# A hybrid decoder trunk: the first norm computed on raw rows and by column groups, the second mixer's rows loaded in steps, two clearings moved

## Chip, core and metric

The kernel runs on one core of a Trainium2 chip as one program. Its time is the device time of that core in microseconds (us), the median of several executions; lower is better. All five compute engines and their DMA queues run their own instruction lists and meet through semaphores.

## What is computed

One layer of a decoder trunk over 1072 tokens of width 1024: 16 meta and 1024 prompt tokens as one sequence, and 8 decoding sequences of 4 tokens. An RMS norm, one wide input projection, four token mixers (HGRN2, RWKV-7, GLA, mLSTM), a gated sum of their projections, an output projection, and an MLP. In outline:

```
h    = x * rsqrt(mean(x*x) + 1e-6) * norm_mix
z    = h @ w_in                       # 1024 x 7704: mixer inputs and gates
o_b  = mixer_b(z), b = 0..3           # chunkwise recurrences with states in and out
x   += (sum_b sigmoid(z_gate_b) * (o_b @ w_branch_b)) @ w_out
hn   = rms(x, norm_mlp);  x += relu(hn @ w_up)**2 @ w_down
y    = rms(x, norm_final)
```

The change touches the first two lines, and in the mixers only the order of loads and of two clearings. `norm_mix` is a factor per channel and the root a factor per token, so both can be applied on either side of a product with `w_in`.

## The kernel before

Activations lie transposed: 8 rows (k = 0..7) of 128 channels by W = 1074 token columns, in three column groups of 358. A **chunk** is a product of all 8 rows with 128 output columns of the weights. TensorE does each product in float32 by three passes of a faster format (`three`, L477): both operands are split into a high part (a rounded copy) and a low part (the difference). A row of a chunk is 3 groups x 3 passes = 9 matmuls. Weights come through a ring of two slots (u = 0, 1); SyncE loads a slot once TensorE has finished its last chunk, ScalarE makes the high part (`weight_hi`, L467), GpSimd the low part in place (`weight_lo`, L472). Chunk u = 0 accumulates in PSUM banks 0 to 2 and u = 1 in 3 to 5; ScalarE copies them out (`evac`, which releases `banks_free`). Plain float32 products count as two passes each in the profile.

**The start.** SyncE loads constants, the 8 rows of x, the small weights WS (68 output columns: GLA's gate input and mLSTM's two gates), ring slot 0, the masks as float32 (into the second half of tile OT), the other constants and ring slot 1. ScalarE squares each row into four buffers used in turn (`rms_act`), VectorE adds them by two, TensorE sums over channels with a matrix of ones, 12 matmuls (`rms_pe`, L567), and ScalarE forms the root RST of all 1074 columns (L614, L616). Only then VectorE scales row after row by `norm_mix` and RST (L2061), ScalarE makes its high part (L1611), VectorE its low part (L627). TensorE does for each row first the small projection (L1035, three float32 matmuls) and then the row of chunk 0, then the whole of chunk 1. ScalarE copies the small projection into GA, passes the first barrier, makes the high part of chunk 2's weights (L467), four operations on mLSTM's gate rows (L1637 to L1641), and copies chunk 0 out (L1631 to L1633). Chunk 2 starts once chunk 0's banks are free and its weights split.

**The rows of the second mixer** (GLA and HGRN2 together). While mLSTM's tiles run, further chunks are filled in on TensorE column group by column group (`fill_work`; `fill_out` copies each group out of PSUM banks 6 and 7, and a whole row goes to the DRAM scratch `proj`). GpSimd's DMA queue brings the rows back: two first, then, when row 9 has been stored, the other eight at once behind the stores of mLSTM's states, and then tile after tile of v (`load_v`).

**Tiles and clearings.** The second mixer runs over 8 tiles of 128 tokens and a tail that also holds the decoding sequences. In each tile GpSimd prepares for TensorE a product by head for each of 7 levels (`gl_by_head`, L861, L863) and a weight's low part in between. After tile 4 it clears SGL (9 segments x 512 columns, the states of the tail) and issues 8 loads of states. In the RWKV mixer it clears RSTL (9 x 256) during the second tile, then loads states.

Of the kernel before, what the change touches and what calls it, by code (L numbers as in the profile page):

```python
# [55 lines left out]
def constants():  # L56
# [52 lines left out]
    xr xr_ready y_done y_out y_ready rows0 rows1 rows2 rows3 zeroed  # L109
# [32 lines left out]
def build(nc, A, OUT, fcols, ucols, fdim, udim):  # L142
    ctx = ExitStack()
    with ctx:
# [55 lines left out]
        def col(name, j=0, rows=P, lo=0):  # L200
            o, _ = COLS[name]
            return CC[lo:rows, o + j:o + j + 1]
# [62 lines left out]
        SQB = OT[:, 0:4]  # L265
        CUF = OT[:, 4:KD].rearrange("p k t -> p (k t)")[:, 0:udim]
# [15 lines left out]
        EMM = a.take(t=TILES + 1, h=4)  # L282
        MC = a.take(s=4, t=P)
# [4 lines left out]
        MATT = a.take(h=4, t=P)  # L288
        MKH = a.take(c=P)
# [145 lines left out]
        SUMS_OF_6 = KD - 1 + KD // 2 + 5  # L435
# [127 lines left out]
        def rms_pe(e):  # L563
            for i in range(KD // 2):
                e.wait_ge(S("norm_sum"), i + 1)
                for g in range(3):
                    last = e.matmul(PS(g, 0, GRP), ones, SQB[:, (2 * i) % 4, g * GRP:(g + 1) * GRP],  # L567
                                    start=i == 0, stop=i == KD // 2 - 1)
                last.then_inc(S("sq_used"), 1)

        def sum_pe(e, n, sq, bank):

            e.wait_ge(S("norm_sum"), n * (KD - 1) + KD // 2)
            for g in range(3):
                last = e.matmul(PS(bank + g, 0, G2), ones, sq[:, 0, part2(g)], start=True, stop=True)
            last.then_inc(S("sq_used"), 1)

        def group_sum_pe(e, g):

            e.wait_ge(S("norm_sum"), SUMS_OF_6 + (2, 4, 5)[g])  # L580
            if g == 2:
                e.wait_ge(S("rstd"), 3)
            last = e.matmul(PS(6 + g % 2, 0, G2), ones, SQ3[:, 0, part2(g)], start=True, stop=g < 2)
            if g == 2:
                e.wait_ge(S("norm_sq"), 2 * KD + 6 + 2 * (g + 1))
                last = e.matmul(PS(6, 0, G2), ones, SQ4[:, part2(g)], start=False, stop=True)
            last.then_inc(S("sq_used"), 1)

        def square(e, sq, n, k, src):

            if k >= 2:
                e.wait_ge(S("norm_sum"), (n - 1) * (KD - 1) + k - 1 + KD // 2)
            e.activation(sq[:, min(k, 1), T2], src[:, T2], ACT.Square, scale=D ** -0.5).then_inc(S("norm_sq"), 1)

        def add_square(e, sq, n, k):

            e.wait_ge(S("norm_sq"), n * KD + k + 1)
            if k > 1:
                e.wait_ge(S("norm_sum"), (n - 1) * (KD - 1) + k - 1 + KD // 2)
            e.tensor_tensor(sq[:, 0, T2], sq[:, 0, T2], sq[:, 1, T2], ALU.add).then_inc(S("norm_sum"), 1)  # L600

        def rms_act(e, st):
            for k in range(KD):
                e.wait_ge(S(f"x{k // 2}"), 32)
                if k >= 4:
                    e.wait_ge(S("sq_used"), (k - 4) // 2 + 1)
                e.activation(SQB[:, k % 4], XT[:, k, :], ACT.Square, scale=D ** -0.5).then_inc(S("norm_sq"), 1)
# [87 lines left out]
        def _(e):  # L695
# [5 lines left out]
            e.dma_start(WS, A["w_small"]).then_inc(S("ws"), 16)  # L701
# [55 lines left out]
        def pool_program(e):  # L757
# [12 lines left out]
            for u in range(2):  # L770
                weight_lo(e, u, P_ML)
# [78 lines left out]
            def gl_by_head(n, w, halves, between=None):  # L850
# [3 lines left out]
                for l in range(1, len(halves) + 1):  # L854
# [10 lines left out]
                    if l == 3 and between is not None:  # L865
                        between()
            def gl_tile(n):
                gl_by_head(n, P, HALVES, lambda: weight_lo(e, 1, n + (P_FILL + Q_GL_TILES)))
# [69 lines left out]
            e.wait_ge(S("rw_copied"), 3)  # L938
            e.memset(RSTL, 0.0).then_inc(S("zeroed"), 1)
# [71 lines left out]
            for g in range(3):  # L1011
                for v, sq in enumerate((SQ3[:, 1], SQ4)[:1 if g == 2 else 2]):
                    e.wait_ge(S("norm_sq"), 2 * KD + 6 + 2 * g + v + 1)
# [13 lines left out]
        def _(e):  # L1027
            e.wait_ge(S("consts"), 32)
            rms_pe(e)

            e.wait_ge(S("ws"), 64)
            for k in range(KD):
                e.wait_ge(S("ht_ready"), k + 1)
                for g in range(3):
                    last = e.matmul(PS(3 + g, 0, GRP)[0:68], WS[:, k, :], XT[:, k, g * GRP:(g + 1) * GRP],  # L1035
                                    start=k == 0, stop=k == KD - 1)
                if k == KD - 1:
                    last.then_inc(S("small"), 1)
                if k == 0:
                    e.wait_ge(S("split0"), P_ML + 1)  # L1040
                e.wait_ge(S("ot_ready"), k + 1)
                for g in range(3):
                    last = three(e, PS(g, 0, GRP), 0, k, slice(g * GRP, (g + 1) * GRP), k == 0, k == KD - 1)
            last.then_inc(S("chunk_done0"), 1)
            arrive(e)

            pe_chunk(e, 1, P_ML, P_ML)
# [508 lines left out]
            e.wait_ge(S("rstd"), 2)  # L1556
# [47 lines left out]
        def _(e):  # L1604
# [4 lines left out]
            for k in range(KD):  # L1609
                e.wait_ge(S("ht_ready"), k + 1)  # L1610
                e.activation(HT_R[:, k], XT[:, k, :], ACT.Copy).then_inc(S("hi_parts"), 1)  # L1611
            weight_hi(e, 1, P_ML)
            e.wait_ge(S("small"), 1)
            e.activation(row3(GA[0:16, :]), cols3(3)[0:16], ACT.Copy)
# [1367 lines left out]
```

## Time and profile before

| | |
|---|---|
| median of 3 executions (lowest, highest) | 2144.61 us (2144.0, 2159.99) |
| profiled execution, its own time | 2163.3 us |
| its span, first to last instruction | 2161.3 us |
| mean granted clock of TensorE | 0.978 of 2.4 GHz |
| TensorE busy | 2077.3 us (96%), 15235 matmul instructions |
| VectorE busy | 1032.9 us (48%) |
| ScalarE busy | 607.2 us (28%) |
| GpSimd busy | 453.9 us (21%) |
| DMA | 177.96 MB, mean 82 GB/s |

PE is TensorE's matmuls, PEld its weight loads, DVE VectorE, ACT ScalarE, POOL GpSimd, SP SyncE; a q behind a name is that engine's sequencer or DMA queue. L477 is line 477 of the kernel. An idle time is put down to what released the instruction after it. Tile names are the program's allocations: AR is the large arena that holds x, the root and the mixers' tiles, CF the constants, PS the PSUM.

### The profile page before, as it was taken

How to read it: one execution, taken by the hardware profiler on the slowest of the kernel's cores; microseconds unless marked ns; L12 is line 12 of the kernel's file. 1: busy time of each engine (PE TensorE's matmuls, PEld its weight loads, DVE VectorE, ACT ScalarE, POOL GpSimd, SP SyncE). 2: the span in 40 equal slices, each digit the busy share in tenths (PEclk: the TensorE clock that was granted, in tenths of full speed). 3: DMA queues.
4: the chain of work that ended last, by engine and by line, in shares of the span. 5: the costliest groups of instructions: out<-in, count | busy, mean ns of one | idle time of the engine just before them, and what ended most of it. 6: DMA issues, size and time to landing. Idle time of an engine off the chain costs nothing.

```text
span 2161.3 us, 37070 instructions
## 1 busy us (share of the span) xinstructions
PE 2077.3 (96%) x15235; PEld 1967.6 (91%) x15235; DVE 1032.9 (48%) x1616; ACT 607.2 (28%) x821; POOL 453.9 (21%) x463
## 2 busy tenths in 40 slices
PE   6999999999999989998899899999999999999997
PEld 4999988999999878887789899999999999999996
DVE  4052333465655545454443685522222235565656
ACT  4432224332322254222222431101011023333343
POOL 1122113444653511100002572200000010000020
PEclk9999999999999989999998999999999999999999
DMA  4123225222221332111024662311111242111112
GB/s 169 40 61 85 60 90 163 81 69 65 65 66 64 132 113 80 32 42 42 22 61 150 218 194 87 111 57 49 39 49 59 89 168 101 49 44 44 49 39 100
DMA packets 50852, 177.96 MB, mean 82 GB/s; under 512 B 6481, under 2 KB 10033, under 8 KB 50497
## 3 DMA queue, kind: packets, MB, share of 16 engines
q1 hardware_dynamic: 25296, 85.77, 13.7%
q0 software_dynamic: 17648, 61.31, 8.3%
q10 hardware_dynamic: 7808, 29.41, 3.7%
q8 instruction: 81, 1.33, 0.3%
q14 instruction: 19, 0.15, 0.0%
HBM read 128.95 MB, written 47.51 MB: 82 GB/s over the span
## 4 chain that ended last, share of the span: by engine, by line
PE 85%; DVE 7%; issue 3%; DMA 3%; ACT 2%; POOL 0%; DVEq 0%; SPq 0%; ACTq 0%; POOLq 0%
PE PS L477 29%; PE PS L649 22%; PE PS L1565 16%; PE PS L1537 2%; PE PS L1172 2%; DMA RING<-in_w_all 1%; DVE AR L2602 1%; DMA RING<-in_w_br 1%; PE PS L1184 1%; PE PS L1035 1%; PE PS L1207 1%; PE PS L1200 1%; DVE CF_parts L623 1%; PE PS L1253 1%; PE PS L1292 0%
## 5 line engine op out<-in xcount | busy, mean ns | idle before, releaser
L477 PE MATMUL PS<-HT_parts,WHIA_parts 128*128 128x352 f32 (+1 forms) x1440 | 517.1, 359 | 12.3 <-POOL RING_parts L472 6.6
L477 PE MATMUL PS<-OT_parts,WHIA_parts 128*128 128x352 f32 (+1 forms) x1440 | 477.5, 332 | 0.0
L477 PE MATMUL PS<-HT_parts,RING_parts 128*128 128x352 f32 (+1 forms) x1440 | 476.5, 331 | 0.0
L472 POOL TENSOR_TENSOR RING_parts<-RING,WHIA_parts 128x1024 fp32r<-128x1024 f32 x60 | 160.6, 2676 | 711.8 <-ACT WHIA_parts L467 711.8
L477 PEld LDWEIGHTS PS<-HT_parts,WHIA_parts 128*128 128x128 f32 x1440 | 279.4, 194 | 29.0 <-issue 12.7
L477 PEld LDWEIGHTS PS<-OT_parts,WHIA_parts 128*128 128x128 f32 x1440 | 279.8, 194 | 4.0 <-issue 0.5
L477 PEld LDWEIGHTS PS<-HT_parts,RING_parts 128*128 128x128 f32 x1440 | 279.2, 194 | 0.0
L1565 PE MATMUL PS<-MIXHI_parts,CF_parts 128*128 128x352 f32 x786 | 253.8, 327 | 5.0 <-DVEq L2852 3.0
L649 PE MATMUL PS<-HT_parts,CF_parts 128*128 128x352 f32 x768 | 249.4, 325 | 0.9 <-ACT AR L616 0.9
L649 PE MATMUL PS<-HT_parts,RING_parts 128*128 128x352 f32 x768 | 249.5, 325 | 0.0
L649 PE MATMUL PS<-OT_parts,CF_parts 128*128 128x352 f32 x768 | 249.2, 325 | 0.0
L1565 PE MATMUL PS<-MIXHI_parts,RING_parts 128*128 128x352 f32 x768 | 248.7, 324 | 0.0
L1565 PEld LDWEIGHTS PS<-MIXHI_parts,CF_parts 128*128 128x128 f32 x786 | 147.6, 189 | 8.4 <-DVEq L2852 2.6
L2007 ACT ACTIVATE MIXHI_parts<-AR 128x1056 fp32r<-128x1056 f32 x94 | 102.2, 1088 | 166.3 <-PE PS L1565 160.6
L649 PEld LDWEIGHTS PS<-HT_parts,CF_parts 128*128 128x128 f32 x768 | 144.9, 189 | 1.3 <-ACT AR L616 1.2
L649 PEld LDWEIGHTS PS<-OT_parts,CF_parts 128*128 128x128 f32 x768 | 145.0, 189 | 0.1
L649 PEld LDWEIGHTS PS<-HT_parts,RING_parts 128*128 128x128 f32 x768 | 144.8, 189 | 0.0
L1565 PEld LDWEIGHTS PS<-MIXHI_parts,RING_parts 128*128 128x128 f32 x768 | 144.3, 188 | 0.0
L2811 DVE SCALAR_TENSOR_TENSOR AR<-PS,AR 128x1056 f32 (+1 forms) x32 | 40.3, 1258 | 191.0 <-PE PS L649 184.5
L1565 PE MATMUL PS<-CF_parts 128*128 128x352 f32 x378 | 122.8, 325 | 0.0
L1565 PE MATMUL PS<-LO_parts,CF_parts 128*128 128x352 f32 x372 | 120.1, 323 | 0.0
L623 DVE CAST CF_parts<-RING 128x1024 fp32r<-128x1024 f32 x80 | 63.2, 789 | 103.7 <-DMA RING<-in_w_all 80.4
(453 smaller groups left out, 3321.5 us busy)
## 6 DMA issues: line engine op xcount, KB each, us to landing
RING<-in_w_all SPq DMA_DIRECT2D x132, 512.0 KB, 3.7
AR<-gates POOLq DMA_DIRECT2D x32, 528.0 KB, 4.0
proj<-AR ACTq DMA_DIRECT2D x18, 537.0 KB, 5.3
AR<-proj POOLq DMA_DIRECT2D x18, 537.0 KB, 7.7
gates<-CF ACTq DMA_DIRECT2D x16, 528.0 KB, 5.3
gates<-AR ACTq DMA_DIRECT2D x16, 528.0 KB, 5.7
AR<-in_xT SPq DMA_DIRECT2D x8, 537.0 KB, 8.4
AR<-in_xT POOLq DMA_DIRECT2D x8, 528.0 KB, 5.5
```

Of the source, the lines that this page charges most:

```text
L472: e.tensor_tensor(RING_R[:, u], RING[:, u], WHIA_R[:, u].bitcast(F32), ALU.subtract).then_inc(S(f"split{u}"), 1)
L477: last = e.matmul(out, a_[:, u, k, :], b_[:, k, t], start=first and i == 0, stop=end and i == 2)
L623: return e.tensor_copy(hi, x)
L649: last = e.matmul(PS(3 * u + g, 0, G2), a_[:, u, k, :], b_[:, k, t], start=k == 0 and i == 0, stop=k == KD - 1 and i == 2)
L1035: last = e.matmul(PS(3 + g, 0, GRP)[0:68], WS[:, k, :], XT[:, k, g * GRP:(g + 1) * GRP], start=k == 0, stop=k == KD - 1)
L1172: last = e.matmul(PS(3 * (l % 2), lo * m, hi * m)[0:w], x[:, g, l, 0:w], GQB[:, l % 2, lo * m:hi * m], start=True, stop=True)
L1184: last = e.matmul(PS(3 * (l % 2) + b, c * w, c * w + w)[0:w], x[r, g, nl + 1, 0:w], q[r, g, 1, 0:w], start=True, stop=True)
L1200: e.matmul(PS(3, h * 64, h * 64 + 64)[0:w], att[:, ao:ao + w], v[:, h * 64:h * 64 + 64], start=h == 0, stop=False, skip_group_check=True)
L1537: last = e.matmul(PS(3 * u + tg, 0, G2), a_[:, v, k, :], b_[:, k, t], start=k == 2 * br and i == 0, stop=k == 2 * br + 1 and i == 2)
L1565: last = e.matmul(PS(3 * v + g, 0, G2), a_[:, u, 4 * v + r % 4, :], b_[:, part2(g)], start=r == 0 and i == 0, stop=r == 31 and i == 2)
L2007: e.activation(AHI_R[r % 2][:, T2], act_row(r)[:, T2], ACT.Copy).then_inc(S("act_hi"), 1)
L2811: e.scalar_tensor_tensor(row2(dst), cols2(3 * u), 0.0, row2(RST2), ALU.max, ALU.mult).then_inc(S(f"banks_free{u}"), 1)
```

## The change

Six edits. (1) WS is scaled by `norm_mix` and the small projection runs on the raw rows, four of them before the sums over channels and four behind; its result is multiplied by the root afterwards. (2) The squares have a buffer each; VectorE adds them up in two trees, the last row in three column groups, so that TensorE needs 6 matmuls with ones instead of 12; the root is formed group by group. (3) TensorE does rows 0 to 4 of chunk 0, then rows of chunk 1 and chunk 0 by turns; the low parts of the first two ring slots move from GpSimd to VectorE; both slots and WS are loaded earlier, the masks go in two pieces to another place. (4) Six of the eight rows of the second mixer are loaded by two and two before and between other work, two are left behind the wait. (5) SGL is cleared in thirds inside tile 5 and its states are loaded behind that tile; tiles 6 and 7 are written out instead of looped. (6) The clearing of RSTL waits for the second RWKV tile's solved values (`rw_us`). Renumbered semaphore counts and the new places of the masks are left out here. In the diff `small(k)` is the small projection of row k and `row(u, k)` the nine matmuls of row k of a chunk; `clear_segments` is called behind levels 4, 5 and 6 of tile 5; VectorE scales row 0 in three groups, each behind its part of the root.

```diff
@@ helpers
+        SQB = [OT[:, k] if k < 4 else HT[:, k] for k in range(KD)]
+        SQ_SUM = SQB[0], SQB[4]
...
+        def rms_pe(e, part):
+            if part == 0:
+                e.wait_ge(S("norm_sum"), 3)
+                for g in range(3):
+                    e.matmul(PS(g, 0, GRP), ones, SQ_SUM[0][:, g * GRP:(g + 1) * GRP], start=True, stop=False)
+                return
+            for g in range(3):
+                e.wait_ge(S("norm_sum"), 4 + 2 * (g + 1))
+                e.matmul(PS(g, 0, GRP), ones, SQ_SUM[1][:, g * GRP:(g + 1) * GRP],
+                         start=False, stop=True).then_inc(S("sq_used"), 1)
...
         def rms_act(e, st):
-            for k in range(KD):
+            for k in range(KD - 1):
                 e.wait_ge(S(f"x{k // 2}"), 32)
-                if k >= 4:
-                    e.wait_ge(S("sq_used"), (k - 4) // 2 + 1)
...
+            for g in range(3):
+                t = slice(g * GRP, (g + 1) * GRP)
+                e.activation(SQB[KD - 1][:, t], XT[:, KD - 1, t], ACT.Square, scale=D ** -0.5).then_inc(S("norm_sq"), 1)
             weight_hi(e, 0, P_ML)
-            e.wait_ge(S("sq_used"), KD // 2)
-            rstd(e, st, row3(RST), cols3(0)).then_inc(S("rstd"), 1)
+            for g in range(3):
+                e.wait_ge(S("sq_used"), g + 1)
+                rstd(e, st, RST[:, g * GRP:(g + 1) * GRP], PS(g, 0, GRP)).then_inc(S("rstd"), 1)
+
+        def rms_sums(e):
+            def add(a_, b_, t=slice(0, W)):
+                e.tensor_tensor(SQB[a_][:, t], SQB[a_][:, t], SQB[b_][:, t], ALU.add).then_inc(S("norm_sum"), 1)
+            for i in range(2):
+                e.wait_ge(S("norm_sq"), 2 * i + 2)
+                add(2 * i, 2 * i + 1)
+            e.wait_ge(S("norm_sum"), 2)
+            add(0, 2)
+            e.wait_ge(S("norm_sq"), 6)
+            add(4, 5)
+            for g in range(3):
+                t = slice(g * GRP, (g + 1) * GRP)
+                e.wait_ge(S("norm_sq"), KD + g)
+                add(6, 7, t)
+                e.wait_ge(S("norm_sum"), 4 + 2 * g + 1)
+                add(4, 6, t)
@@ SyncE
             for k in range(KD):
                 e.dma_start(XT[:, k, :], xs[k]).then_inc(S(f"x{k // 2}"), 16)
-            e.dma_start(WS, A["w_small"]).then_inc(S("ws"), 16)
+                if k == 0:
+                    e.dma_start(WS, A["w_small"]).then_inc(S("ws_in"), 16)
...
             load(0, A["w_all"], 0)
-            e.dma_start(CUF, A["cu"]).then_inc(S("ws"), 16)
+            load(1, A["w_all"], 1)
             e.dma_start(CF[:, first:], A["cf"][:, first:]).then_inc(S("ws"), 16)
-            load(1, A["w_all"], 1)
+            e.dma_start(CUF0, A["cu"][:, 0:CU_CUT]).then_inc(S("ws"), 16)
+            e.dma_start(CUF1, A["cu"][:, CU_CUT:]).then_inc(S("ws"), 16)
@@ GpSimd
-            for u in range(2):
-                weight_lo(e, u, P_ML)
             arrive(e)
...
             e.wait_ge(S("states_final"), 1)
+            for u in range(2):
+                e.wait_ge(S(f"fill_sent{u}"), (Q_RW - 1) * 16)
+            for i, dst in ((6, GQ[:, 2]), (7, GK[:, 2])):
+                e.dma_start(dst, proj_row(i)).then_inc(S("rows1"), 16)
+            for i, slot in ((4, 0), (5, 1)):
+                e.dma_start(OTG[:, slot], proj_row(i)).then_inc(S("rows2"), 16)
             for h in range(4):
...
+            for i, dst in ((0, GQ[:, 0]), (1, GQ[:, 1])):
+                e.dma_start(dst, proj_row(i)).then_inc(S("rows1"), 16)
             weight_lo(e, 1, P_FILL + Q_RW)
             for u in range(2):
                 e.wait_ge(S(f"fill_sent{u}"), Q_RW * 16)
-            for i, slot in ((4, 0), (5, 1), (8, 2), (9, 3)):
+            for i, slot in ((8, 2), (9, 3)):
                 e.dma_start(OTG[:, slot], proj_row(i)).then_inc(S("rows2"), 16)
-            for i, dst in ((0, GQ[:, 0]), (1, GQ[:, 1]), (6, GQ[:, 2]), (7, GK[:, 2])):
-                e.dma_start(dst, proj_row(i)).then_inc(S("rows1"), 16)
...
             with e.Fori(0, 5) as n:
                 gl_tile(n)
-            e.memset(SGL, 0.0).then_inc(S("zeroed"), 1)
+            def clear_segments(i):
+                if i < 3:
+                    ins = e.memset(SGL[:, 3 * i:3 * i + 3], 0.0)
...
+            gl_tile(5, clear_segments)
             e.wait_ge(S("zeroed"), 5)
             load_states()
-            with e.Fori(5, TILES - 1) as n:
+            for n in range(6, TILES):
                 gl_tile(n)
-            gl_tile(TILES - 1)
...
             e.wait_ge(S("rw_copied"), 3)
+            e.wait_ge(S("rw_us"), 2)
             e.memset(RSTL, 0.0).then_inc(S("zeroed"), 1)
@@ TensorE
+            e.wait_ge(S("ht_ready"), 1)
+            for k in range(4):
+                small(k)
+            rms_pe(e, 0)
+            rms_pe(e, 1)
+            for k in range(4, KD):
+                small(k)
             arrive(e)
-            pe_chunk(e, 1, P_ML, P_ML)
+            for k in range(5):
+                row(0, k)
+            for k in range(5, KD):
+                row(1, k - 5)
+                row(0, k)
+            e.wait_ge(S("ws"), 64)
+            for k in range(3, KD):
+                row(1, k)
@@ ScalarE
             for k in range(KD):
-                e.wait_ge(S("ht_ready"), k + 1)
+                e.wait_ge(S("ht_ready"), k + 2)
                 e.activation(HT_R[:, k], XT[:, k, :], ACT.Copy).then_inc(S("hi_parts"), 1)
+                if k == 2:
+                    weight_hi(e, 1, P_ML)
+                if k == 3:
+                    e.wait_ge(S("small"), KD)
+                    e.activation(row3(GA[0:68, :]), cols3(3)[0:68], ACT.Copy).then_inc(S("banks_free1"), 1)
@@ VectorE
+            e.wait_ge(S("ws_in"), 16)
+            e.tensor_tensor(WS, WS, bc(col("norm_mix", 0, P, 0, KD).unsqueeze(2), WS.shape), ALU.mult).then_inc(S("ht_ready"), 1)
+            rms_sums(e)
+            weight_lo(e, 0, P_ML)
...
             for k in range(KD):
+                e.wait_ge(S("small"), k + 1)
...
                 if k == 4:
+                    weight_lo(e, 1, P_ML)
             h_lo(KD - 1)
+            e.wait_ge(S("banks_free1"), 1)
+            e.tensor_tensor(GA[0:68, :], GA[0:68, :], RST[0:68, :], ALU.mult)
```

## Rows read from the trace of the kernel before

**Rows 1.** Waits of TensorE (line, tile, releaser: us in total, times, longest us)
```profile
PE PS L477 <- POOL RING_parts L472: 6.6, 2, 4.4
...
PE PS L1385 <- DVE AR L2607: 5.0, 8, 2.5
...
PE PS L477 <- ACTq L1618: 2.0, 1, 2.0
```

**Rows 2.** Chain that ended last, 0 to 60 us (start us, us, what)
```profile
2.39 6.19 DMA AR<-in_xT
...
12.22 3.45 PE PS L567 x6
...
27.11 3.82 PE PS L1035 x6
...
33.00 1.81 PE PS L1035 x6
...
34.81 1.48 PE PS L477 x9
...
57.95 2.12 PE PS L477 x10
```

**Rows 3.** Timeline, 44 to 100 us (start us, us, engine, line, operation [idle before])
```profile
56.17 51.18 SPq L704 DMA_DIRECT2D RING<-in_w_all  x5
...
66.26 0.21 ACT L1633 ACTIVATE AR<-PS 128x32 f32<-128x32 f32 x1
...
71.58 0.77 ACT L1631 ACTIVATE AR<-PS 128x716 f32<-128x716 f32 x1 [5.12 <-PE PS L477]
```

**Rows 4.** Timeline, 0 to 44 us
```profile
11.40 2.09 ACT L607 ACTIVATE OT<-AR 128x1074 f32<-128x1074 f32 x2 [0.71 <-DMA AR<-in_xT]
...
29.32 1.33 DVE L2061 SCALAR_TENSOR_TENSOR AR<-AR,CC 128x1074 f32<-128x1074 f32 x1
...
31.76 1.33 DVE L2061 SCALAR_TENSOR_TENSOR AR<-AR,CC 128x1074 f32<-128x1074 f32 x1
```

**Rows 5.** Windows of 1 us (busy us and instructions by engine, granted clock, DMA)
```profile
60.00:61.00 1.00, 1.00 (x5) 1.00 (x4) 0.00 (x0) 0.97 (x2) 0.21 (x1) 0.50 0.00 0
```

**Rows 6.** Chain that ended last, 340 to 400 us
```profile
360.59 12.50 DMA RING<-in_w_all
...
376.65 23.45 PE PS L477 x132
```

**Rows 7.** DMA issues, 318 to 425 us (count, KB each, median us to landing)
```profile
AR<-proj POOLq DMA_DIRECT2D x8, 537.0 KB, 13.4
...
RING<-in_w_all SPq DMA_DIRECT2D x6, 512.0 KB, 4.4
```

**Rows 8.** Timeline, SyncE's queue, 318 to 425 us
```profile
346.58 73.52 SPq L704 DMA_DIRECT2D RING<-in_w_all  x6
```

**Rows 9.** Timeline, VectorE and GpSimd, tiles of the second mixer
```profile
386.08 0.43 DVE L2304 COPY AR<-AR 128x384 f32<-128x384 f32 x1
...
566.14 0.77 POOL L861 TENSOR_TENSOR AR<-AR,CF 128x128 f32<-128x128 f32 x2 [0.99 <-PE PS L1172]
...
583.00 3.98 POOL L879 MEMSET AR<- 128x4608 f32 x1
...
585.50 1.76 DVE L2304 COPY AR<-AR 128x384 f32 x1
```

**Rows 10.** Timeline, VectorE, GpSimd and ScalarE, second and third RWKV tiles
```profile
902.84 4.76 DVE L2602 COPY AR<-AR 32x128 f32<-32x128 f32 x4
...
904.96 2.11 POOL L939 MEMSET AR<- 128x2304 f32 x1
...
916.68 0.39 ACT L1920 ACTIVATE AR<-PS 128x256 f32<-128x256 f32 x1 [6.85 <-PE PS L1400]
...
936.90 3.03 DVE L2602 COPY AR<-AR 32x128 f32<-32x128 f32 x4
```

**Rows 11.** Chain that ended last, whole span
```profile
965.92 2.26 DVE AR L2602
```

More of the change, by code:

```diff
@@ L198, in mask8, with col @@
             return CU[0:rows, o + k * w:o + (k + 1) * w]
-        def col(name, j=0, rows=P, lo=0):
+        def col(name, j=0, rows=P, lo=0, n=1):
             o, _ = COLS[name]
-            return CC[lo:rows, o + j:o + j + 1]
+            return CC[lo:rows, o + j:o + j + n]
         ZS = CF[:, fcols["bd_ml"][0]:fcols["bd_ml"][0] + W]
@@ L282, in build @@
         EMM = a.take(t=TILES + 1, h=4)
+        CU_CUT = 4 * P + 4 * P + P + 4 * P + 4 * P
+        CUF0 = Arena(a.at).take(c=CU_CUT)
         MC = a.take(s=4, t=P)
@@ L288, in build @@
         MATT = a.take(h=4, t=P)
+        CUF1 = Arena(a.at).take(c=udim - CU_CUT)
         MKH = a.take(c=P)
@@ L561, in evac @@
             emit(3 * u).then_inc(S(f"banks_free{u}"), 1)
-        def rms_pe(e):
-            for i in range(KD // 2):
-                e.wait_ge(S("norm_sum"), i + 1)
+        def rms_pe(e, part):
+            if part == 0:
+                e.wait_ge(S("norm_sum"), 3)
                 for g in range(3):
-                    last = e.matmul(PS(g, 0, GRP), ones, SQB[:, (2 * i) % 4, g * GRP:(g + 1) * GRP],
-                                    start=i == 0, stop=i == KD // 2 - 1)
-                last.then_inc(S("sq_used"), 1)
+                    e.matmul(PS(g, 0, GRP), ones, SQ_SUM[0][:, g * GRP:(g + 1) * GRP], start=True, stop=False)
[4 more added lines that the diff above has]
+                         start=False, stop=True).then_inc(S("sq_used"), 1)
         def sum_pe(e, n, sq, bank):
-            e.wait_ge(S("norm_sum"), n * (KD - 1) + KD // 2)
+            e.wait_ge(S("norm_sum"), n * (KD - 1) + SUMS0)
             for g in range(3):
@@ L864, in gl_by_head, with gl_tile, between @@
                                     ALU.mult).then_inc(S("gl_qb"), 1)
[L865 to L868, printed above, removed]
+                    if between is not None:
+                        between(l)
+            def gl_tile(n, clear=None):
+                def between(l):
+                    if l == 3:
+                        weight_lo(e, 1, n + (P_FILL + Q_GL_TILES))
+                    elif l > 3 and clear is not None:
+                        clear(l - 4)
+                gl_by_head(n, P, HALVES, between)
                 weight_lo(e, 0, n + (P_FILL + Q_GL_TILES + 1))
@@ L1028, in _, with small @@
             e.wait_ge(S("consts"), 32)
-            rms_pe(e)
-            e.wait_ge(S("ws"), 64)
-            for k in range(KD):
-                e.wait_ge(S("ht_ready"), k + 1)
+            def small(k):
+                e.wait_ge(S(f"x{k // 2}"), 32)
                 for g in range(3):
@@ L1036, in _, with row @@
                                     start=k == 0, stop=k == KD - 1)
-                if k == KD - 1:
[L1038 to L1044, printed above, removed]
-            arrive(e)
-            pe_chunk(e, 1, P_ML, P_ML)
+                last.then_inc(S("small"), 1)
+            def row(u, k):
+                if u == 0:
+                    e.wait_ge(S("ot_ready"), k + 1)
+                if k == 0:
+                    e.wait_ge(S(f"split{u}"), P_ML + 1)
+                    if u == 1:
+                        e.wait_ge(S("banks_free1"), P_ML + 1)
+                for g in range(3):
+                    last = three(e, PS(3 * u + g, 0, GRP), u, k, slice(g * GRP, (g + 1) * GRP), k == 0, k == KD - 1)
+                if k == KD - 1:
+                    last.then_inc(S(f"chunk_done{u}"), 1)
+            e.wait_ge(S("ht_ready"), 1)
[5 more added lines that the diff above has]
+                small(k)
+            arrive(e)
+            for k in range(5):
[6 more added lines that the diff above has]
+                row(1, k)
             for p in range(P_ML + 1, P_FILL):
@@ L2805, in _ @@
                     split_chunk(e, u, i + P_OUT + 1)
[L2807 removed]
+            e.wait_ge(S("rstd"), 4)
             def relu(i, u, dst):
```

64 lines of the change are left out of this document (29 added, 35 removed).

## The prediction

> **What bounds the kernel now.** I read part 1 of the page first: TensorE is busy 96% of the span, so an edit is worth only what it takes out of TensorE's own waiting, the slow matmuls behind such a wait, or matmuls. Then the list of TensorE's waits [rows 1], to see which waits the diff touches, and last the chain and the timeline at each such place. There are four: the start, where few matmuls run until the norm is known [rows 2]; the hand-over from chunk 0 to the next ones; a ring load that arrives late beside the mixer's rows; and the two clearings on GpSimd. The chain that ends last leads through TensorE at all four, and behind each of them TensorE's order is full again, so time saved there comes off the end.
>
> **The sum's base.** The profiled execution took 2163.3 us, its span 2161.3; the median of the three runs is 2144.6, 18.7 less. The gains below come from the profiled one, and I take them off the median unscaled.
>
> **Part 1, the start.** Before, the chain is: rows land, squares, adds, 12 ones-matmuls, root, scaling, and only then small projection and chunk 0 by turns, 1.81 + 1.48 us a row [rows 2]. Chunk 1 ends when its copy can start, at 71.6 [rows 3]. I work out the same point for after.
> Rows land: the first pair at 8.6 (2.39 + 6.19) [rows 2], the second at 11.4 [rows 4], so 2.8 us a pair. The small weights (272 KB, half a row) now stand behind row 0 and push all by 0.8: 9.4, 12.2, 15.0, 17.8. Two squares take 2.09 [rows 4], so seven and three thirds end at 20.1; the DVE adds of the last row come in thirds (two of about 0.5 each, an estimate by size from the 1.33 of a whole row's scaling [rows 4]), so the three sums are ready at 20.4, 21.5 and 22.5. TensorE meanwhile does small(0 to 3) from 9.4: at the slow pace 3.45 us hold six passes, at the fast one 1.81 [rows 2], so 3.6 + 3 x 1.8 = 9.0, till 18.4; six ones-matmuls follow, the last ending at 23.2, then small(4 to 7), 4 x 1.81, till **30.45**. The DVE does not wait for that: after the last third of the root (about 24.3) it scales row 0, and ScalarE's copy and the low part make it ready at 27.8; each next one costs 2.44 (31.76 - 29.32) [rows 4]: rows 1 to 3 at 30.3, 32.7, 35.2. The low part of ring 1, now on DVE (about 1.2, by size from the same 1.33), puts row 4 at 38.8. TensorE does rows 0 to 3 till 36.6, waits 2.2, and then has two chunks to draw on: five and three rows of chunk 0, with three of chunk 1 between, till 49.25; the five left of chunk 1 till 56.65. The drop of the clock behind a wait of 2 us is seen before: after 2.0 of it [rows 1], from 57.95, the eight rows of chunk 1 should take 8 x 1.48 = 11.8 and took 13.6 [rows 2, 3], with 0.50 granted at 60 (1.2 GHz of 2.4) [rows 5]. I charge 1.5 for the wait of 2.2: chunk 0 ends at 50.75.
> What is late next: chunk 2 needs chunk 0's banks. Before, the load issued at 56.2, ScalarE's high part, four 4-row operations and three copies followed one another until 66.5, 10.5 after chunk 0's end (57.95 - 2.0) [rows 1 to 3]; that was hidden under chunk 1, whose 12 us are now cut to 7.4. So chunk 2 starts at 50.75 + 10.5 = 61.25 after a wait of about 3, plus another 1.5 of slow matmuls: 62.75 against 71.6. **Gain 8.8.** Bounds: 11.8 with no drop at all, 1 if the slow pace holds through small(0 to 3) and the ones (about 8 more). I take the middle reckoning because the clock did rise within the first six passes before.
> The other edits here: WS's scaling on DVE (about 0.7) lies before the sums; scaling GA by the root (1.27) and the mask copy in two parts move to DVE's end, at about 48, before ScalarE needs the barrier; POOL is released from two low parts. Cost 0 under that cover, at most 2.5 without. SP issues both ring loads ahead of the constants, which are wanted from 47 on only.
>
> **Part 2, the second mixer's rows.** The ring load issued at 360.6 took 12.5 us [rows 6], against a median of 4.4 for the six of this stretch, while eight rows of 537 KB took a median of 13.4 [rows 7]. TensorE waited 4.4 for the low part behind it [rows 1] and then ran slow for about 12 matmuls; as above that is 1.6. After, four rows are issued at about 346 and two behind the state stores, and only rows 8 and 9, the tile of v, the load and one store (about 2.4 MB) are under way at 360.6, against 5.7 MB before. In proportion the load takes 12.5 x 2.4/5.7 = 5.3, lands at 366, say 367 with what is left of the state stores, and its chunk is ready 3.6 later (376.65 - 373.09) [rows 6], at 370.6; TensorE wants it 4.4 before 376.65, at 372.2. **Gain 6.0**, bounds 0 and 6.0.
> Queued behind it: on POOL the six row issues (about 0.55 each) stand before the low part of ring 1. That chunk's load starts at 346.6 [rows 8] and now shares with four rows and a store, 3.3 MB: at 5.7 MB in 12.5 us it lands near 354 instead of 351, and the chunk is ready at 357.6. It is wanted three column groups (8 x 1.48/3 = 3.95 each) ahead of 372.2, at 360.4, so it fits, by almost 3 us. ScalarE waits those 3 us and has no work that TensorE wants before. DVE's wait for the rows becomes shorter.
> The Trainium skill (DMA: Bandwidth & Descriptors, Queues, rings and completion order) says that a DMA engine goes round robin between the queues. By that rule the ring load has a third of the engines whatever the number of rows, and the sum would lose this term. The 12.5 us speak against it here.
>
> **Part 3, clearing SGL.** The whole clearing took 3.98 on GpSimd, and DVE's copy of 128x384 took 1.76 beside it, 0.43 elsewhere [rows 9]; the norm that TensorE transposes next stands behind that copy on DVE, so the 1.3 are TensorE's. In thirds of 1.33 it falls beside DVE's predicated copies from PSUM. At level 7 GpSimd idles 0.99 waiting for TensorE [rows 9], so the three pieces eat the slack and push a little. Bounds of the push 0 and 4.0; I take 0.3, since idle time stands before levels 6 and 7. **Gain 1.0.** The eight state loads (5 us of issuing) move behind tile 5, where the weight's low part and the same issue stood before; the states are wanted in the tail only.
>
> **Part 4, clearing RSTL.** It ran 904.96 to 907.07, and DVE's four small copies took 4.76 beside it, against 3.03 in the next tile [rows 10]. TensorE's wait was 2.5 where the eight tiles together have 5.0 [rows 1], and the tile lasted 34.06 (936.90 - 902.84) against 29.02 for the next (965.92 - 936.90) [rows 10, 11]: 2.0 of waiting and 3.0 of slow clock. Held until the second tile's RUS, it runs from 917.1 (916.68 + 0.39) to 919.2 [rows 10]. **Gain 5.0**, bounds 2 and 5.0. GpSimd's next work is the low part of a later weight, over 10 us off.
> The Trainium skill (SBUF — State Buffer, Who interferes with whom) says that a GpSimd instruction and a DVE copy or tensor_scalar with both ports exclude each other for its whole length. The trace agrees (4.76 against 3.03). By it a small DVE operation at 919.0 would wait 0.2.
>
> **Sum.** 8.8 + 6.0 + 1.0 + 5.0 = 20.8; the profiled execution would be 2142.5, the median **2123.8**.
>
> **Rivals.**
> - *The start gives little*: the slow pace lasts, or the chain to chunk 0's banks waits longer. For it: slow matmuls from 12.2 and again from 27.1 [rows 2]. Against: a rise each time. It gives 1 to 4 instead of 8.8: 2130. Chance 0.14.
> - *The ring load stays slow*: what delays it is any traffic on GpSimd's queue, and 1.3 MB is still issued there at 359. Against: it is a quarter of before. 2123.8 + 6.0 = 2129.8. Chance 0.12, the skill's rule in it.
> - *More than reckoned*: the hand-over drops no clock and row 4 is not waited for. 2123.8 - 3.0 = 2120.8. Chance 0.15.
> - *The clearings find a new victim*: thirds push levels 5 to 7, or the held one blocks DVE's tail work. 3 to 5 lost: 2128. Chance 0.07.
> - *The clock stays down through the start* (slower). DVE feeds a row each 2.44 us and TensorE needs 1.48, 61% busy. Should that keep 1.2 GHz until chunk 1 ends, every pass costs double from 9.4 on: smalls 2 x 14.5, ones 7.2, 16 rows at 2.7: about 88.6, which is 17 later than 71.6 rather than 8.8 earlier: 2123.8 + 25.8 = 2149.6. It decides once more than about 20 us of the gain go. Against: 2.4 GHz came back after 3.8 us at 27.1. Chance 0.03.
> - *Nothing is changed in effect*: 2144.6. Chance 0.02.
> The forecast keeps 0.47, own range 2118 to 2129.
>
> **Numbers.** The range reaches from the better case to the single losses and holds four cases in five: 2116 to 2132. One per cent of 2144.6 is 21.4, about what a measurement of this kernel can tell, so faster by over 1% means below 2123.2: the better case and a bit under half of the forecast, since it lies 0.6 from the line: 0.41. Slower by over 1%: 0.03. Within: 0.56.
>
> **What would show it.** Small projection on TensorE from about 9.4; chunk 2's first matmul at 61 to 63, behind a wait of about 3 us for ScalarE; no wait of over 1 us for a low part near 370 and a ring load of 5 to 7 us; DVE's copy at the sixth tile of GLA back at 0.43; the second RWKV tile at 29 us. Wrong if TensorE waits instead for the root, for a ring load near 355, or for the products by head.

## The result, and the profile after

| | kernel before | changed kernel |
|---|---|---|
| median of the comparison | 2152.1 us (10 runs, 2140.8 to 2160.0) | 2136.4 us (10 runs, 2128.7 to 2143.4) |
| profiled execution / its span | 2163.3 / 2161.3 | 2138.1 / 2136.5 |
| granted clock over the span | 0.978 | 0.983 |

The ratio is 0.9945, 95% interval 0.9925 to 0.9964: 11.8 us less (8 to 16), where 20.8 were forecast; the two medians lie 15.7 apart, inside that interval. Timed again later, the same kernel gave 0.995 (0.9926 to 0.9974). One execution of the kernel u2 below (2154.9 us) was in a slower state and is left out of its ratio. The two profiled executions lie 25 us apart, more than the medians, because the one of before was 11 us above its own median; so where single traces are compared below, several kernels with the same part stand side by side.

**The start.** From the chain of waits of the changed kernel, 0 to 62 us (start us, us, what):

```profile
9.80 10.35 PE PS L1079 x24
20.15 1.81 PE PS L572 x6
...
39.65 10.66 PE PS L481 x63
50.33 0.06 SPq L733
...
50.50 3.46 DMA RING<-in_w_all
...
60.54 0.09 ACT AR L1694
60.63 0.14 issue
60.77 1.23 PE PS L481 x3
```

The small projection (L1079) runs from 9.8; before, there was only waiting and twelve ones-matmuls until 27.1 [rows 2]. Chunk 0 ends at 50.3 (50.75 forecast), chunk 2's first matmul is at **60.77** (61.25 forecast; the step stood at 71.6 before [rows 3]).

**Waits of TensorE** (line, tile, releaser: us in total, times, longest us), which answer to [rows 1]:

```profile
PE PS L481 <- POOL RING_parts L476: 5.8, 2, 5.3
...
PE PS L481 <- ACT AR L1694: 3.1, 1, 3.1
PE PS L1448 <- DVE AR L2678: 3.0, 8, 0.6
```

The clearing of RSTL no longer costs TensorE a wait (2.5 longest before, 0.6 now). The wait for chunk 0's banks (3.1) was reckoned with. The first row speaks against the forecast: the wait for a low part near 370 was to vanish, and it grew from 4.4 to 5.3.

**The second mixer's rows.** The chain, 340 to 380 us, answers to [rows 6]:

```profile
351.21 13.35 DMA RING<-in_w_all
...
365.73 2.35 POOL RING_parts L476
368.08 0.04 issue
368.12 11.95 PE PS L481 x55
```

The ring load took 13.35 us, not the 5.3 of the forecast, though two rows and not eight are issued near it. By windows of 4 us (busy us and instructions of PE, PEld, DVE, ACT, POOL; granted clock, DMA share, GB/s):

```profile
344.00:348.00 4.00, 4.00 (x26) 4.00 (x26) 0.00 (x0) 2.06 (x4) 3.98 (x5) 1.00 1.20 393
348.00:352.00 4.00, 4.00 (x26) 4.00 (x25) 1.11 (x1) 3.34 (x5) 2.30 (x4) 1.00 1.28 57
352.00:356.00 4.00, 4.00 (x27) 4.00 (x26) 3.28 (x3) 3.56 (x3) 0.00 (x0) 1.00 0.75 38
356.00:360.00 4.00, 4.00 (x26) 4.00 (x25) 0.00 (x0) 0.00 (x0) 0.00 (x0) 1.00 0.90 331
```

From 348 to about 357 the DMA engines are reported busy and move 38 to 57 GB/s, a tenth of the 393 to 410 before and after. This **slow stretch** is the row to read: the ring load was not waiting for bytes ahead of it, everything was slow. What moved in 2 us of it, and in 2 us behind it (queue: packets, MB, share of 16 engines):

```profile
q0 software_dynamic: 16, 0.06, 80.0%
...
q0 software_dynamic: 154, 0.59, 72.9%
q1 hardware_dynamic: 31, 0.13, 16.3%
q10 hardware_dynamic: 25, 0.11, 13.0%
```

The first row is 352 to 354: GpSimd's queue alone (q0), each packet more than 1 us long, while the ring load (q1) and a filler store (q10) had been issued near 351 and moved nothing. The other three rows are 358 to 360. In the records of single packets the packets of the first row are the row loads' own, some 4 KB each; each of the four stores of state n (elements of 4 bytes) appears as 16 packets of 72 bytes, and these went out between 347.2 and 355.5.

**The clearing of RSTL** (start us, us, engine, line, operation), second RWKV tile, answers to [rows 10]:

```profile
893.65 2.96 DVE L2673 COPY AR<-AR 32x128 f32<-32x128 f32 x4
...
902.86 2.02 POOL L985 MEMSET AR<- 128x2304 f32 x1 [7.02 <-ACT AR L1981]
...
923.19 2.33 DVE L2673 COPY AR<-AR 32x128 f32<-32x128 f32 x1
```

DVE's copies take 2.96 instead of 4.76; the tile lasts 923.19 - 893.65 = 29.5 us instead of 34.1. At the sixth tile of GLA DVE's copy of 128x384 takes 0.41 (at 578.1; 0.43 forecast), and the three pieces of SGL are cleared behind it, from 593.0 to 599.7.

### The profile page after: what moved, and what is told of

Same layout as the page of the kernel before. It is cut to its first block, busy times and chain, and to the rows that moved or that the text cites. A ratio compares the mean times of both kernels' runs of the same rounds, so it can differ in the third digit from the quotient of the medians.

```text
span 2136.5 us, 37031 instructions
## 1 busy us (share of the span) xinstructions
PE 2067.6 (97%) x15223; PEld 1959.4 (92%) x15223; DVE 1038.5 (49%) x1629; ACT 605.1 (28%) x825; POOL 443.1 (21%) x463
## 4 chain that ended last, share of the span: by engine, by line
PE 85%; DVE 8%; DMA 3%; issue 2%; ACT 2%; DVEq 0%; POOL 0%; SPq 0%; ACTq 0%
PE PS L481 29%; PE PS L677 22%; PE PS L1628 16%; PE PS L1600 2%; PE PS L1235 2%; DMA RING<-in_w_all 1%; DVE AR L2673 1%; PE PS L1247 1%; DMA RING<-in_w_br 1%; PE PS L1270 1%; DVE OT_parts L655 1%; PE PS L1263 1%; DVE CF_parts L651 1%; PE PS L1316 1%; PE PS L1406 1%
## 5 line engine op out<-in xcount | busy, mean ns | idle before, releaser
L481 PEld LDWEIGHTS PS<-HT_parts,WHIA_parts 128*128 128x128 f32 x1440 | 278.2, 193 | 31.3 <-issue 12.6
L476 POOL TENSOR_TENSOR RING_parts<-RING,WHIA_parts 128x1024 fp32r<-128x1024 f32 x58 | 150.7, 2599 | 695.7 <-ACT WHIA_parts L471 695.7
L608 POOL TENSOR_TENSOR AR<-AR 128x1056 f32<-128x1056 f32 x12 | 29.4, 2449 | 392.5 <-ACT AR L601 392.5
```

The lines of the kernel that those rows point to most:

```text
L476: e.tensor_tensor(RING_R[:, u], RING[:, u], WHIA_R[:, u].bitcast(F32), ALU.subtract).then_inc(S(f"split{u}"), 1)
L481: last = e.matmul(out, a_[:, u, k, :], b_[:, k, t], start=first and i == 0, stop=end and i == 2)
```

## The experiments

The question: why did the ring load stay slow, and what is each part worth? Theory **H1**: the mLSTM's state stores (c, 32 x 9 pieces of 256 bytes for each head, and n, 32 x 9 elements of 4 bytes for each head; GpSimd's queue, just before) make the slow stretch. Rival **H2**: the row loads on that queue do.

**Chunk 0's banks first.** In ScalarE's order:

```diff
-            weight_hi(e, 0, P_ML + 1)
             e.wait_ge(S("zeroed"), 2)
 ...
+            evac(e, 0, 0, pre_conv(0))
+            weight_hi(e, 0, P_ML + 1)
             e.activation(RI, GA[32:36, :], ACT.Copy)
 ...
-            evac(e, 0, 0, pre_conv(0))
```

> The changed kernel, with ScalarE's copies of chunk 0's banks put ahead of the high part of the next weight and of the gate rows' four small operations. Theory: chunk 2's start is bound by ScalarE's order alone (load landed 53.98, high part, four small operations, three copies till 60.6), and TensorE's wait of 3.1 us there costs itself and some 3 us of slow clock in the chunks behind it. Then the copies end near 52.5, the low part of the weight near 57.5, the wait before chunk 2 falls to under 0.5 us, and the first transposes of the mLSTM, at 115.0 in the changed kernel, come at 109 to 112; the time is 3 to 6 us under the changed kernel's. Rival: the wait is for the weight's load and its low part on GpSimd (57.4), which come no earlier: the wait stays over 2 us, the transposes come at 115.

Measured: ratio to the kernel before 0.9897 (0.9836 to 0.9959). TensorE runs through; its chain from 45 us on:

```profile
44.88 64.08 PE PS L481 x389
108.96 1.97 PE PS L1123 x18
```

The transposes come at 109.0 against 115.0. The six us are the 3.1 of waiting and 3 of slow clock behind it. Over the ten traces that keep ScalarE's old order behind the changed start the transposes stand at 111.5 to 114.8, over the three with the new one at 108.8 to 109.2, so 2.5 to 6 is the fair figure. The theory holds at this place; the time agrees and says no more (0.0048 below the changed kernel's ratio, some 10 us, but from four runs, with an interval that holds the changed kernel's 0.9945).

**Is it the stores?** Four kernels, one profiled run each. The first leaves state c and n out but for eight pieces:

```diff
-  e.dma_start(OUT["mc"][:, h].rearrange("s k v -> k s v"), SML[r, :, h * 65:h * 65 + 64])...
-  e.dma_start(OUT["mn"][:, h].rearrange("s k -> k s"), SML[r, :, h * 65 + 64])...
+  e.dma_start(OUT["mc"][0:1, h, 0], SML[32 * h:32 * h + 1, 0, h * 65:h * 65 + 64])...
+  e.dma_start(OUT["mn"][0:1, h], SML[32 * h:32 * h + 1, 0, h * 65:h * 65 + 32])...
```

> The changed kernel without the mLSTM's state stores: each of the eight (four of c, whose pieces are 256 bytes, four of n, whose elements go out singly, 4 bytes each) is replaced by one piece of one partition, so that the counts stay; the states c and n of the output are left out. H1, the scattered stores slow the DMA engines for some 6 us and the ring load behind them waits for that: the ring load issued near 351 lands within 4 to 7 us instead of 13.35, TensorE's wait of 5.3 us for the low part goes to under 0.5, and its order from there on comes 5 to 7 us earlier. H2, the row loads issued on GpSimd's queue just before the ring load hold it back: it stays at 12 to 14 us. H1 also says that the loads of rows 4 to 7, issued ahead of the stores, land as before, and rows 0, 1, 8, 9 earlier by 5 us or more.

A miss: ring load 11.2 us, TensorE's wait 3.1. A slow stretch was there with eight tiny stores (1.5 KB in all), from about 346 to 350, shorter and less deep (73 to 159 GB/s by windows of 1 us).

The second stores state n in longer pieces:

```diff
-  e.dma_start(OUT["mn"][:, h].rearrange("s k -> k s"), SML[r, :, h * 65 + 64])...
+  e.dma_start(OUT["mn"][:, h], SML[32 * h:32 * h + 1, :, h * 65:h * 65 + 32])...
```

> The changed kernel with only the four stores of state n changed: 9 pieces of 128 bytes from one partition each, instead of 288 elements of 4 bytes (the values stored there are not n). If the 4-byte elements are what slows the engines, the ring load near 351 lands within 4 to 8 us, as without any of the stores. If the 1152 pieces of 256 bytes of state c are, it stays above 10. If H2 holds (the row loads before it), it stays at 12 to 14.

Ring load 6.2 us, TensorE's wait behind it 0.3. The windows of this kernel, for the ones above:

```profile
344.00:348.00 4.00, 4.00 (x26) 4.00 (x25) 0.00 (x0) 2.49 (x3) 4.00 (x6) 1.00 1.04 398
348.00:352.00 4.00, 4.00 (x26) 4.00 (x25) 2.69 (x3) 3.36 (x5) 0.67 (x1) 1.00 1.02 412
352.00:356.00 4.00, 4.00 (x27) 4.00 (x26) 3.76 (x8) 2.11 (x3) 0.00 (x0) 1.00 0.82 308
```

The same bytes, the same rows ahead of the load, the same 1152 pieces of 256 bytes of state c, and no slow stretch. Only the 4-byte pieces are gone (4 stores of 32 x 9 elements, 4.6 KB together). So it is these. The third holds three of the loads on GpSimd's queue back:

```diff
-            for i, slot in ((8, 2), (9, 3)):   # and load_v(0), ahead of the ring load
+            e.wait_ge(S("chunk_loaded0"), (P_FILL + Q_RW + 2) * 16)
+            for i, slot in ((8, 2), (9, 3)):
```

> The changed kernel with rows 8 and 9 and the first tile of v issued on GpSimd only once the ring load has landed; the state stores stay ahead of it. H1 (the scattered stores slow the engines): the ring load issued near 351 finds the same slow stretch and lands in 9 to 12 us, shorter only by the share that rows 8, 9 and v take after it; TensorE's wait stays over 2 us. H2 (row loads on GpSimd's queue issued shortly before it): it lands in 4 to 6 us and the wait is gone.

12.3 us, a little over H1's 9 to 12; TensorE waits 5.9. Six rows still stand ahead of the load here, so this run alone clears rows 8, 9 and v; it is the run before (e3), with every row load in its place and no slow stretch, that makes H2 fall. The fourth stores neither c nor n:

```diff
-  both state stores; the four waits on their count lowered by 8 x 16
```

> The changed kernel with none of the eight mLSTM state stores (c and n of the states are left out of the output), and the counts waited for lowered to match. The run that put one piece of one partition in place of each store kept a slow stretch (11.2 us for the ring load), the run that stored n in pieces of 128 bytes had none. If the slow stretch is made by stores whose data goes out 4 bytes at a time, and a single piece of one partition is cut up just so, then here the row loads move at over 400 GB/s from 345 on, the ring load issued near 350 lands in 4 to 7 us and TensorE's wait for the low part stays under 0.6. If the slow stretch has another cause (the rows read shortly after they were written, or the row loads themselves), it stays, and the load takes over 10 us.

7.3 us, a little over the 4 to 7 expected, with 417 to 421 GB/s from 345 to 350; TensorE's wait behind it is 0.3, as expected, though GpSimd took 3.4 us for that low part instead of 2.35. From 340 to 352, packets of the kernel with one piece for each store, then of this one:

```profile
DMA packets 1085, 3.18 MB, mean 265 GB/s; under 512 B 347, under 2 KB 347, under 8 KB 1084
...
DMA packets 1155, 4.39 MB, mean 366 GB/s; under 512 B 129, under 2 KB 129, under 8 KB 1154
```

That explains the miss. The records of single packets show what the eight pieces became: against the kernel without stores there are 64 more packets of 16 bytes, 64 more of 8 and 128 more of 4 (16 for each store, as for the other transfers of this queue). So a piece of a single partition was cut in 16, 256 bytes into 16 and 128 bytes into 8, and packets of 8 and 16 bytes made a slow stretch too, where the n stores of e3 went out as packets of 128 bytes and made none. What lies between 16 and 128 bytes was not tried, and why so few bytes slow everything stays open.

**What is each part worth?** Five kernels, each timed several times beside the kernel before.

```diff
 u1: parts 2, 3 and 4 undone (the start alone)
 u2: part 2 undone (all eight rows behind the stores and the low part)
 u34: parts 3 and 4 undone
   e.wait_ge(S("fill_sent..."), (Q_RW - 1) * 16)
-  rows 6, 7, 4, 5
   the eight state stores
+  rows 6, 7, 4, 5          (x7: stores first)
```

> Part 1 of the change alone: the rows of the second mixer, and both clearings, are as in the kernel before. If the start gives what the trace of the changed kernel shows (chunk 2 at 60.8 instead of 71.6, less some 3 us of slow clock behind the wait there), the time is 7 to 9 us below the kernel before (ratio 0.996), with the ring load near 351 at 12 to 14 us. Rival: the start's gain is eaten on the way, by waits for transfers that don't come earlier; then under 4 us are left (ratio over 0.998).

> The changed kernel with part 2 undone: all eight rows of the second mixer are issued behind the state stores and the low part again. If part 2 brought nothing, since the slow stretch behind the stores is what the ring load waits for, the time is that of the changed kernel within 2 us (ratio to the kernel before 0.993 to 0.996), with the ring load at 12 to 14 us. If the number of row loads matters beside it, as the prediction had it, the ring load takes over 15 us here and the time is 3 to 6 us above the changed kernel's (ratio 0.996 to 0.998).

> The changed kernel with parts 3 and 4 undone: SGL is cleared in one piece behind tile 4's loop, RSTL as soon as its place is free. By the traces the two are worth 1.9 and 4.6 us: the time is 5 to 8 us above the changed kernel's (ratio 0.997 to 0.999 to the kernel before), TensorE's waits for DVE are back (2.5 to 2.9 us longest, at the second tile of RWKV, and 1.3 to 2.9 at the sixth of GLA). Rival: the waits move elsewhere when removed, and the two are worth under 3 us.

> The changed kernel with rows 6, 7, 4 and 5 issued behind the eight state stores instead of ahead of them. Theory M: part 2 did not shorten the ring load because its four rows (2.1 MB) stand ahead of the stores on GpSimd's queue and push the 4-byte elements of n from 340 to 348 to 357, into the time of the ring load issued near 350. With the stores first the slow stretch is over by about 347, the ring load takes 6 to 10 us, TensorE's wait for the low part is under 2 us, and the time is 5 to 9 us below the changed kernel's (ratio to before 0.989 to 0.992). Rival: six rows issued before the ring load cost it as much as the slow stretch does (M is wrong, the bytes count); then it stays at 12 us or more and the time at the changed kernel's.

> The changed kernel itself, on the chip of the next three, so that they can be compared with it directly. Ratio to the kernel before 0.993 to 0.997, as measured before.

| kernel | median us | ratio to the kernel before, 95% |
|---|---|---|
| changed kernel again (same chip as x7, u34) | 2137.0 | 0.9950 (0.9926 to 0.9974) |
| u1: start alone | 2142.8 | 0.9976 (0.9954 to 0.9997) |
| u2: change without part 2 | 2123.4 | **0.9902** (0.9866 to 0.9937) |
| u34: change without the clearings | 2146.1 | 1.0000 (0.9975 to 1.0026) |
| x7: change with the stores first | 2127.1 | **0.9906** (0.9869 to 0.9943) |

The clearings were worth a little more than expected (9.1 by the medians, 5 to 8 expected), with TensorE's waits for DVE back at 2.9 in both loops; the start alone was worth a little less (5.5 for 7 to 9), and its ring load took 8.2, not 12 to 14. The third row is a surprise that both theories of that run missed: without part 2 the kernel is some 9 us *faster* ((0.9945 - 0.9902) x 2150; the two intervals overlap a little). x7 gives as much on the same chip (2137.0 - 2127.1 = 9.9; these two intervals overlap a little as well), by turning the order of twelve DMA issues. The ring load took 9.1 in u2 and 10.0 in x7, where u2's two theories had 12 to 14 and over 15. In x7 (its windows):

```profile
344.00:348.00 4.00, 4.00 (x27) 4.00 (x26) 0.67 (x1) 3.71 (x5) 4.00 (x6) 1.00 0.80 41
348.00:352.00 4.00, 4.00 (x26) 4.00 (x25) 3.73 (x3) 3.62 (x3) 0.23 (x1) 1.00 0.83 231
352.00:356.00 4.00, 4.00 (x27) 4.00 (x25) 0.00 (x0) 0.02 (x1) 0.00 (x0) 1.00 1.02 420
```

The stores go out at 334 to 339, the slow stretch lies at 340 to 349, the ring load issued at 347.6 takes 10.0, and TensorE's longest wait for the low part is 1.9. In the changed kernel four rows (2.1 MB) stand ahead of the stores on their queue and hold the 4-byte pieces back until about 347: part 2 carried the slow stretch into the ring load. The last n store lands at about 358 in the changed kernel (issued at 342.9, 15.4 us) and at about 349 in u2 (338.6, 10.8 us), and in both full speed comes back within 1 us of that. (x7's own late guest is ScalarE's silu, which waits 4.6 for rows issued into the slow stretch.)

One stretch shows it over fourteen traces: from the first matmul of the gate projection behind the mLSTM (L1206) to the first product of GLA tile 0 (L1235), both by their first start:

```
before                                              56.0
change; again; u34; banks first; rows 8, 9, v held  58.0  58.6  58.7  58.5  58.5
part 2 undone: u1; u2                               54.3  51.1
stores first: x7                                    54.3
eight tiny stores                                   53.2
no 4-byte pieces there (e3, e5 and two candidates)  50.4  50.3  50.4  51.2
```

Part 2 costs 4 to 7 us beside the changed start; with part 2 in, the 4-byte pieces cost 8. The rows cost something by themselves as well: in the second candidate below, with eight rows at once and no slow stretch (321 to 425 GB/s), the ring load takes 9.1 us and TensorE waits 1.1, in e3 6.2 and 0.3.

The clearings by tile. GLA, from the fourth tile to the sixth, around the clearing of SGL, by DVE's L2434: 77.3, 77.2 and 78.8 us where it runs in one piece (before, u1, u34), 74.6 or 74.7 in ten of the eleven others. Of the 77.3, only one belongs to the clearing: the tile that it disturbs lasts 38.5 there against 37.4 in the ten, and the other 1.6 lie in the tile ahead, whose clock is low (0.83 granted over 570 to 580) before the clearing begins at 583.0. In u1 and u34, where TensorE waits 2.9 and not 1.3, the disturbed tile lasts 40.0 and 41.6. RWKV, from the first tile to the third, by L2678: 63.1, 68.6 and 66.4 against 58.3 to 62.8 (mean 59.6). So part 3 is worth 1 to 4 us and part 4 from 3.5 to 9, both least in the trace of before; the timed difference of u34 (9 to 12 us) lies within their sum.

**Candidates.**

```diff
 chunk 0's banks first, and
-  e.dma_start(OUT["mn"][:, h].rearrange("s k -> k s"), SML[r, :, h * 65 + 64])   (POOL, x4)
+  ins = e.tensor_copy(MNK[r, :], SML[r, :, h * 65 + 64])                         (DVE, x4)
+  e.dma_start(OUT["mn"][:, h].rearrange("s k -> k s"), MNK[32 * h:32 * h + 32, :])
+      (POOL, one behind each of three later low parts, one before GLA tile 5)
```

> A candidate: the changed kernel with chunk 0's banks copied ahead of the next high part, and with state n copied by DVE into a small tile of its own (128x9), from which GpSimd stores it one quarter at a time, behind the low parts of three later weights and before tile 5 of GLA. Theory: the four n stores together slow all transfers for some 9 us; one at a time costs 2 to 3 us of transfers each, which no ring load with 8 us to spare feels. Then the ring load near 345 lands in 5 to 7 us, TensorE's wait for the low part (5.3 us) and the slow clock behind it go, and the time is 9 to 13 us below the changed kernel's (ratio to the kernel before 0.988 to 0.991). Rival: the waits only move, to the ring loads beside the later n stores (loads of 8 us or more and new waits for low parts at 365 to 400); then the gain over the changed kernel is only the 4 to 6 us of the copies' order.

> A candidate: the start and both clearings of the change, chunk 0's banks copied first, state n stored a quarter at a time from a tile of its own, and part 2 undone (all eight rows behind the ring load). If rows at full speed cost the ring load nothing worth naming, part 2 is neutral once the n stores are out of the way, and this is within 3 us of the candidate that kept part 2 (ratio 0.985 to 0.989). If the early rows help DVE and ScalarE to finish sooner, it is slower than that one by over 3 us (over 0.989); if they take the ring load's engines, it is faster (under 0.985).

Measured: with part 2 kept 2118.4 us, **0.987** (0.9839 to 0.9902); with part 2 undone 2116.1 us, 0.9884 (0.9839 to 0.9929). Both keep every output and beat both kernels: 16 to 21 us below the changed one, the first with an interval that does not touch its own (0.9925 to 0.9964). The ring load of the story took 8.4 and 9.1 us, longer than the 5 to 7 expected of the first, but no slow stretch lay beside it (235 GB/s or more until the last 2 us), and TensorE's waits there are 0.3 and 1.1. The loads beside the later quarters of n took 6.6 to 7.8 us. With the n stores apart part 2 is neutral, within what these runs tell.

## Why the prediction was wrong

**Part 1, the start: right.** Every station came within 1.3 us up to chunk 2 (small projection 9.8 for 9.4; ones till 22.0 for 23.2; chunk 0's end 50.3 for 50.75; chunk 2 at 60.8 for 61.25). The slow clock fell in behind the wait of 3.1 rather than behind the 1.8 for row 4, and cost 3 where 1.5 + 1.5 were charged. The chunks behind end at 114.8 against 122.6, 7.8 for the 8.8 forecast; timed alone 5.2 (0.6 to 9.9).

**Part 2, the rows: wrong, and this is the failed step:** "In proportion the load takes 12.5 x 2.4/5.7 = 5.3." It took 13.35. A gain of 6.0 was entered and a loss of 4 to 7 came (by the stretch; 9 to 10 by the timed pairs). The proportion took the load for one that waits for other bytes [rows 6, 7]. What the engines moved in that time was not read. From the kernel before, 340 to 385 us in slices of 1.125 us:

```profile
GB/s 0 202 359 408 4 19 77 160 338 344 39 15 49 180 27 1 0 1 34 34 61 111 336 412 422 420 406 410 416 420 420 422 417 399 372 368 168 19 15 0
```

The load was issued at 360.6, in the 19th slice; this one and the next three stand at 34 to 111 GB/s, and only then comes full speed. The slow stretch was there to be seen, 4.5 of the 12.5 us. It too ends with the last n store, issued at 350.11 and landed 14.0 us later:

```profile
350.11 0.61 POOL L811 DMA_DIRECT2D out_mn<-AR  x1
...
out_mn<-AR POOLq DMA_DIRECT2D x1, 1.1 KB, 14.0
```

No run took the n stores out of the kernel before, so for this one the cause is read from the times alone. And the bounds of the term, 0 and 6.0, left out a loss: no row had been read on how the four rows, moved *past the stores*, change when the stores go out. The count of moved DMAs was made for the bytes, not for the order on their own queue. The round robin that the forecast weighed (the Trainium skill, DMA: Bandwidth & Descriptors, Queues, rings and completion order) was rejected with the 12.5 us as witness; the traces now stand by it outside the slow stretch: at 358 to 360 the three queues all move, and at 360 to 362 they share the engines evenly (31 to 35% each). Inside it the ring load got no packet in 6 us while the packets of GpSimd's queue took over 1 us each; how the turns were taken there no run shows.

**Parts 3 and 4, the clearings: right in kind, the size open.** In the trace that the terms were read from they came out: 1.0 for 1.0 at the disturbed tile of GLA, and 3.5 to 4.5 for 5.0 in RWKV. In two other kernels with the clearings in one piece TensorE waited longer (2.9 us each), and there they cost 3 to 4 and 7 to 9; the timed difference is 9 to 12 for the 6.0 forecast.

**The rivals.** "The ring load stays slow" came true (chance 0.12) with another cause, and worse than the 6.0 it would have taken back. Without part 2 the other three terms, 14.8 forecast, measured 21 (0.9902; 14 to 29). Part by part the three measured 14 to 20 (start 5 to 8, clearings 9 to 12). So these terms together were right or up to 6 too small, and one term was wrong by 10 to 16.

**The base** was 2144.6, the median of three runs; of ten it is 2152.1. That is 7.5 us that no step of the working saw. It makes the absolute time look worse (2136.4 for 2123.8, 12.6 off) than the change was (11.8 saved of 20.8, 9.0 off).

## What to carry to other kernels

Before costing a slow transfer by the bytes beside it, read what the engines moved in its time by windows of a few us: here busy engines at a tenth of their GB/s meant small pieces somewhere, and giving those another layout, or another time, one at a time, was the cure. A DMA that is moved ahead of others on the same queue delays them, so ask what they will meet when they come out. And a part that loses in company with three that win is only found by undoing each alone.

## What had not been expected of the hardware

- Four stores of 288 elements of 4 bytes from 32 partitions each, 1.1 KB, slowed all DMA traffic of the core to 38 to 57 GB/s for 8 to 9 us in the changed kernel, until the last of them had landed; 128-byte pieces of the same size in all didn't (398 to 412 GB/s). One such store at a time left ring loads at 6.6 to 7.8 us, where the loads behind them took 4.1 to 4.4.
- Eight pieces of one partition, 128 or 256 bytes each, went out in packets of 8 and 16 bytes and gave a slow stretch of about 4 us (73 to 159 GB/s).
- A wait of 3.1 us of TensorE before chunk 2 cost about 3 us more in slow clock behind it. From 61 to 115 us the granted clock is 0.95 to 0.97 in eight of the ten traces that have the wait and 1.00 in all three that don't (two with the wait have 1.00 as well), so the drop is likely, not certain, behind a wait of this length.
- The largest spread from run to run lies in RWKV's loop: every second tile of the later ones takes 30.7 to 36.7 us and the others 28.9 to 29.3, with waits that nothing in the profile ends:

```profile
PE PS L1378 <- issue: 4.9, 2, 3.8
PE PS L1372 <- issue: 3.9, 3, 2.3
```

They stand where the loop over pairs of tiles goes back to its head. The Trainium skill (Runtime: NRT & Kernel Launch, Instruction fetch mechanics) says that a taken branch to a page not held makes the engine wait for instructions; the rows fit, and no run here tested it by writing the loop out.
